# Loading both halves of a weight tile in one 1 MB transfer, with the raw weight buffers joined into three pairs

## The chip, the cores and the metric

The kernel runs on one core of one Trainium2 chip. Its time is that of the slowest (here the only) core in device microseconds, from one launch with all inputs in HBM to all outputs in HBM. Three runs of the kernel before gave 1528.47, 1528.53 and 1528.87 us; the median is 1528.53 us.

## The reference

Two decoder layers are applied to 288 token rows: 256 new rows of a prompt and 8 x 4 rows of running sequences, with the same weights. Everything is float32.

```python
def layer(x, l, ...):
    x = x + 0.5 * swiglu(rms_norm(x, ffn1_norm[l]), ffn1_w1[l], ffn1_w3[l], ffn1_w2[l])   # 1024 -> 2816 -> 1024
    h = rms_norm(x, mix_norm[l]) @ w_in[l]                     # 1024 -> 6144 columns, read by all three branches
    a_u, a_v, b_q, b_k, b_v, c_q, gates = jnp.split(h, IN_SPLITS, axis=-1)
    y_a = gelu(a_u) * chunk_spatial_gate(layer_norm(gelu(a_v)))
    y_b = moba_attention(rope(b_q), rope(b_k), b_v, paged cache)
    y_c = cross_attention(c_q, mem_k, mem_v)
    x = x + (g_a * (y_a @ w_a) + g_b * (y_b @ w_b) + g_c * (y_c @ w_c)) @ w_o
    x = x + 0.5 * swiglu(rms_norm(x, ffn2_norm[l]), ffn2_w1[l], ffn2_w3[l], ffn2_w2[l])
```

The outputs are the final norm of x and the new keys, values, memory keys and values and gate rows of both layers.

## The kernel before

**Units.** Every weight matrix is cut into tiles of up to 1024 rows by 256 columns, and each tile into two halves, the units. A unit is 128 partitions by 4 row blocks by 256 columns (512 KB); where a tile has 768 or 512 rows, a unit has 3 or 2 row blocks. `layer_units` (its list is `UNITS`) writes the order of a layer's 224 units: 68 of the first FFN, 8 of the memory projection, 24 of `w_in` for queries, keys, values and the gated branch, 40 of gates and branch outputs, 8 of `w_b_out`, 8 of `w_o`, 68 of the second FFN. Units are numbered from 0 to 447 over both layers.

**The way of a unit.** SyncE (SP) loads unit n into raw buffer n % 6 (`load`). ScalarE (ACT) copies it, rounded, into one of four high buffers (`hi`, L831). VectorE (DVE) writes the rest, raw minus high, over the raw data (`lo`, L1158; `wlo` is the same memory as `wraw`). TensorE (PE) multiplies high x high, high x low and low x high: 24 matmuls for a unit of four row blocks (`half`, L476). After its last matmul it raises `w_used`. Four things wait for that count: SP loads unit n when unit n - 6 has been used, ACT rounds unit n when unit n - 4 has been used, and both evacuations of a finished tile start there.

**What sets the order.** Each engine has one program order written out by hand. On ACT the rounding of a later unit stands at a fixed place among the other work; when its data isn't there, everything behind it on ACT waits too. Three places matter below. In the branch part, `slot(i)` is `hi` of the layer's unit 88 + i, so `slot(10)` rounds unit 98 and `slot(14)` unit 102:

```python
            slot(10)
            act.wait_ge(xc_ready, L + 1)
            act.activation(lnsq[:], gv[:], ACT.Square, scale=SGU ** -0.5).then_inc(lnsq_ready, 1)
            ...
            deviation(f"ln2.{L}")
...
            slot(14)
            rows_out("vn", rows_a, 2)
```

`deviation` takes the root that the normalisation of `gv_T` on DVE needs (L1426, L1428), whose rows PE then transposes (L537) and ACT copies back (`rows_out`, L973). In the gate part, step n's sigmoid of unit u stands behind `hi(u + 3)`; the third place is the sigmoid of the layer's unit 123 (branch C, tile 2) behind `hi` of unit 126. The next gate tile uses the same PSUM bank, so PE cannot start unit 126 before that sigmoid is done.

**Pages.** Caches come in as quads of four 256 KB pages. 24 quads of a layer are issued by SP between two weight loads (`quads_after`, at `load_after(q)`), 16 by GpSimd (POOL) on its own queue. Rows of a weight unit are 4 KB per partition, rows of a page are 2 KB.

Of the kernel before, what the change touches and what calls it, by code (L numbers as in the profile page):

```python
# [6 lines left out]
F32 = mybir.dt.float32  # L7
F32R = mybir.dt.float32r
# [5 lines left out]
P = 128  # L14
# [8 lines left out]
W = 256  # L23
# [57 lines left out]
LAYER_UNITS = 224  # L81
# [21 lines left out]
def step_unit(n):  # L103

    return U_GA + sum(1 if k in "ABC" else 2 for k, _, _ in STEPS[:n])


def layer_units():

    def tile(name, t, k0=0, nk=KD):  # L110
        return [(name, t, k0 + h * nk // 2, nk // 2) for h in range(2)]

    def ffn(f):
        u = []
        for i in range(UP):
            u += tile(f"ffn{f}_w1", i) + tile(f"ffn{f}_w3", i)
        for t in range(12):
            u += tile(f"ffn{f}_w2", t // 3, 8 * (t % 3), DOWN_NK[t % 3])
        return u

    def gate(kind, g):
        return tile("w_in", g + (GATE0 + "ABC".index(kind) * D) // W)

    u = ffn(1)
    assert len(u) == U_MEM
    for t in range(4):
        u += tile("w_mem_kv", t)
    for t in [4, 5, 6, 7] + SLOT_TILES:
        u += tile("w_in", t)
    assert len(u) == U_GA  # L130
    for kind, g, h in STEPS:
        u += gate(kind, g)[h:h + 1] if kind in "ABC" else tile(f"w_{kind}_out", g, 0, 4)
    assert len(u) == U_BRB
    for g in range(4):
        u += tile("w_b_out", g, 0, 4)
    for t, h in WO_ORDER:
        u += tile("w_o", t)[h:h + 1]
    assert len(u) == U_FFN2
    u += ffn(2)
    assert len(u) == LAYER_UNITS  # L140
    return u


UNITS = layer_units()
N_UNITS = DEPTH * LAYER_UNITS
NR, NH = 6, 4


def kh_of(n):
    return UNITS[n % LAYER_UNITS][3]  # L150

RES = 48
RES_FFN, RES_MEM, RES_Q, RES_K, RES_TILES, RES_GATE = 13, 2, 1, 1, 4, 4
# [22 lines left out]
def load_after(q):  # L178

    if q in FIRST_LOAD:  # L180
        return FIRST_LOAD[q]
    prev = max(p for p in range(q) if HOMES[p] == HOMES[q])
    free = quad_unit(prev)
    if q == Q_V + 3:
        free = step_unit(13) - 1
    if q == Q_V + 4:
        free = step_unit(14) - 1
    return free + NR


def by_pool(q):
    return 8 <= q < Q_MK or q >= Q_V + 8
# [8 lines left out]
def user_before(L, q):  # L201

    prev = [p for p in range(q) if HOMES[p] == HOMES[q]]
    if prev:
        return QUADS * L + prev[-1] + 1
    return (QUADS * (L - 1) + max(p for p in range(QUADS) if HOMES[p] == HOMES[q]) + 1) if L else 0
# [53 lines left out]
def build(nc, A):  # L260
# [3 lines left out]
    def at(name, shape, dt, offset):  # L264
        return nc.alloc_sbuf_tensor_at(name, shape, dt, offset=offset)

    def room(nbytes):
        o = base[0]
        base[0] += (nbytes + 31) // 32 * 32
        assert base[0] <= 229344, base[0]  # L270
        return o

    def sb(name, shape, dt=F32):
        return at(name, shape, dt, room(int(np.prod(shape[1:])) * 4))

    def sem(name):
        return st.enter_context(nc.semaphore(name))


    wraw, wlo = [], []  # L280
    for u in range(NR):
        o = room(4 * W * 4)
        wraw.append(at(f"wraw{u}", [P, 4, W], F32, o))
        wlo.append(at(f"wlo{u}", [P, 4, W], F32R, o))
    whi = [sb(f"whi{u}", [P, 4, W], F32R) for u in range(NH)]
    x = sb("x_T", [P, KD, T])
    work_at = base[0]
# [80 lines left out]
    raw_loaded = [sem(f"raw_loaded{u}") for u in range(NR)]  # L368
    first_hi, first_lo = sem("first_unit_hi"), sem("first_unit_lo")
    hi_done, lo_done, w_used = sem("hi_done"), sem("lo_done"), sem("w_used")  # L370
# [62 lines left out]
    wt = {n: A[n] for n in TILED}  # L433
# [376 lines left out]
    def _(act):  # L810
# [8 lines left out]
        def hi(n):  # L819

            if n >= N_UNITS:
                return
            kh = kh_of(n)
            act.wait_ge(raw_loaded[n % NR], 16 * (n // NR + 1))
            if n >= NH:
                act.wait_ge(w_used, n - NH + 1)
            if n == 0:
                act.activation(whi[0][:, 0:2, :], wraw[0][:, 0:2, :], ACT.Copy).then_inc(first_hi, 1)
                act.activation(whi[0][:, 2:4, :], wraw[0][:, 2:4, :], ACT.Copy).then_inc(hi_done, 1)
                return  # L830
            act.activation(whi[n % NH][:, 0:kh, :], wraw[n % NR][:, 0:kh, :], ACT.Copy).then_inc(hi_done, 1)  # L831
# [805 lines left out]
    @block.sync  # L1637
    def _(sp):
        nc.disable_value_cache = True

        def load(n):

            name, t, k0, kh = UNITS[n % LAYER_UNITS]
            if n >= NR:
                sp.wait_ge(w_used, n - NR + 1)
            sp.dma_start(wraw[n % NR][:, 0:kh, :], wt[name][n // LAYER_UNITS, t][:, k0:k0 + kh, :])\
                .then_inc(raw_loaded[n % NR], 16)

        def ids_of(i, n):

            G, j = i // 8, i % 8
            _, ids = nc.values_load_multi_w_load_instructions(
                ptab[0:1, :].rearrange("o (b j) -> o b j", j=8)[:, 4 * G:4 * G + 4, j:j + n],
                engines=(mybir.EngineType.SP,), min_val=0, max_val=A["cache_k"].shape[1] - 1)
            return [[ids[e * n + k] for e in range(4)] for k in range(n)]

        held = []

        def quad(L, q):

            b = HOMES[q]
            if user_before(L, q):
                sp.wait_ge(quad_used, user_before(L, q))
            if Q_MK <= q < Q_V:
                cache, i = (cache_mk, q - Q_MK) if q < Q_MV else (cache_mv, q - Q_MV)
                src = [cache[L, 4 * (i // 2) + e, i % 2] for e in range(4)]
            else:
                cache, i = (cache_k, q - Q_K) if q < Q_MK else (cache_v, q - Q_V)
                ids = held[i]
                src = [cache[L, ids[e]] for e in range(4)]  # L1670
            for e in range(4):
                sp.dma_start(page[b][e][:], src[e]).then_inc(page_loaded[b], 16)

        def quads_after(L, n):
            for q in range(QUADS):
                if not by_pool(q) and load_after(q) == n:
                    quad(L, q)

        for g in range(4):
            sp.dma_start(x[:, 2 * g:2 * g + 2, :], A["x_T"][:, 2 * g:2 * g + 2, :]).then_inc(ld_x[g], 16)  # L1680
            if g == 0:
                sp.dma_start(gains[:], A["gains"]).then_inc(ld_gain, 16)
            if g < 2:
                load(g)
        for n in range(2, NR):
            load(n)
        sp.wait_ge(ld_page, 16)
        for L in range(DEPTH):
            b = LAYER_UNITS * L
            for n in range(b + NR if L == 0 else b + NR, b + U_MEM):  # L1690
                load(n)
                if L == 0 and n == 10:
                    sp.dma_start(memn[:], A["mem_T"]).then_inc(ld_mem, 16)
                if L == 0 and n == 14:
                    sp.dma_start(cst[:], A["const"]).then_inc(ld_const, 16)
                if L == 0 and n in (16, 20, 24, 28):
                    held += ids_of(n // 2 - 8, 2)
                if n == b + 28:
                    sp.dma_start(sgb[:], A["sgu_b"][L].unsqueeze(0).broadcast_to([P, 4, P])).then_inc(ld_sb, 16)
                    sp.dma_start(wmT[:], A["sgu_w"][L]).then_inc(ld_sw, 16)  # L1700
                if L and n == b + load_after(0):
                    sp.wait_ge(out_vn, 16 * L)
                    sp.wait_ge(out_v, 32 * L)
                quads_after(L, n - b)
            for n in range(U_MEM, U_BRB):
                load(b + n)
                if n == load_after(2):
                    sp.wait_ge(w_used, b + U_MEM)
                if n == load_after(Q_V + 3):
                    sp.wait_ge(w_used, b + step_unit(13))  # L1710
                if n == load_after(Q_V + 4):
                    sp.wait_ge(*fill(f"O11.{L}"))
                quads_after(L, n)
            for n in range(b + U_BRB, b + LAYER_UNITS + NR):
                if n < N_UNITS:
                    load(n)
        for g in range(4):
            if g == 2:
                sp.wait_ge(y_pool, 1)
            else:  # L1720
                sp.wait_ge(nf_ready, 4 * DEPTH + min(g, 2) + 1)
            sp.dma_start(A["y"][:, 2 * g:2 * g + 2, :], yout[:, 2 * g:2 * g + 2, :]).then_inc(out_y, 16)
        sp.wait_ge(out_y, 64)
# [136 lines left out]
```

## Time and profile before

| | |
|---|---|
| median of three runs | 1528.53 us |
| the profiled execution, its own time | 1527.0 us |
| its span, first to last instruction | 1525.3 us |
| granted TensorE clock, mean | 0.995 |
| PE busy | 1492.3 us (98%) |
| DVE busy, ACT busy, POOL busy | 897.7, 705.5, 103.9 us |
| moved by DMA | 316.03 MB |

The span is 1.7 us shorter than the profiled execution's time, and that execution is 1.5 us shorter than the median of the runs. Busy time of an engine counts its own instructions, not the time in which it waits for a semaphore. A matmul's end is modelled, so a busy PE isn't shown to run at its peak.

### The profile page before, as it was taken

How to read it: one execution, taken by the hardware profiler on the slowest of the kernel's cores; microseconds unless marked ns; L12 is line 12 of the kernel's file. 1: busy time of each engine (PE TensorE's matmuls, PEld its weight loads, DVE VectorE, ACT ScalarE, POOL GpSimd, SP SyncE). 2: the span in 40 equal slices, each digit the busy share in tenths (PEclk: the TensorE clock that was granted, in tenths of full speed). 3: DMA queues.
4: the chain of work that ended last, by engine and by line, in shares of the span. 5: the costliest groups of instructions: out<-in, count | busy, mean ns of one | idle time of the engine just before them, and what ended most of it. 6: DMA issues, size and time to landing. Idle time of an engine off the chain costs nothing. (4 is left out here: it accounts for less than half of the span.)

```text
span 1525.3 us, 28869 instructions
## 1 busy us (share of the span) xinstructions
PE 1492.3 (98%) x12100; PEld 1440.4 (94%) x12100; DVE 897.7 (59%) x1207; ACT 705.5 (46%) x938; POOL 103.9 (7%) x198
## 2 busy tenths in 40 slices
PE   7999999999999999999999999999999999999996
PEld 7999999998878999999999999999988889999995
DVE  6676446656744775555565654665656537655543
ACT  6544335446643454443444443544565435544342
POOL 0000001140012000000000000023100210000000
PEclk9999999999999999999999999999999999999998
DMA  6555659794698544455555466688856955444551
GB/s 241 183 180 190 190 173 322 259 358 155 215 342 292 168 159 165 163 165 162 170 166 176 166 201 181 222 288 301 314 194 208 357 190 199 159 165 162 159 165 66
DMA packets 107026, 316.03 MB, mean 207 GB/s; under 512 B 13392, under 2 KB 13392, under 8 KB 106768
## 3 DMA queue, kind: packets, MB, share of 16 engines
q1 hardware_dynamic: 94320, 273.67, 54.0%
q0 software_dynamic: 12576, 40.51, 7.3%
q8 instruction: 96, 1.57, 0.4%
q14 instruction: 34, 0.28, 0.1%
HBM read 306.00 MB, written 5.77 MB: 204 GB/s over the span
## 5 line engine op out<-in xcount | busy, mean ns | idle before, releaser
L1158 DVE TENSOR_TENSOR wlo<-wraw,whi 128x1024 fp32r<-128x1024 f32 (+2 forms) x447 | 511.0, 1148 | 516.6 <-ACT whi L831 514.9
L476 PE MATMUL res<-norm_hi,whi 128*128 128x288 f32 x2176 | 652.1, 300 | 13.6 <-DVE wlo L1151 7.9
L476 PE MATMUL res<-norm_lo,whi 128*128 128x288 f32 x2176 | 643.3, 296 | 0.0
L831 ACT ACTIVATE whi<-wraw 128x1024 fp32r<-128x1024 f32 (+2 forms) x447 | 441.3, 993 | 433.5 <-PE res L476 361.6
L476 PE MATMUL res<-norm_hi,wlo 128*128 128x288 f32 x2176 | 641.2, 295 | 0.0
L476 PEld LDWEIGHTS res<-norm_hi,whi 128*128 128x128 f32 x2176 | 409.1, 188 | 25.4 <-issue 8.8
L476 PEld LDWEIGHTS res<-norm_hi,wlo 128*128 128x128 f32 x2176 | 411.0, 189 | 0.0
L476 PEld LDWEIGHTS res<-norm_lo,whi 128*128 128x128 f32 x2176 | 410.0, 188 | 0.5
L476 PE MATMUL res<-h_hi,whi 128*128 128x288 f32 x1024 | 304.3, 297 | 1.3 <-DVE h_lo L1597 0.8
L476 PE MATMUL res<-h_lo,whi 128*128 128x288 f32 x1024 | 302.1, 295 | 0.0
L476 PE MATMUL res<-h_hi,wlo 128*128 128x288 f32 x1024 | 301.3, 294 | 0.0
L476 PEld LDWEIGHTS res<-h_hi,whi 128*128 128x128 f32 x1024 | 191.9, 187 | 4.9 <-DVE h_lo L1597 1.7
L476 PEld LDWEIGHTS res<-h_hi,wlo 128*128 128x128 f32 x1024 | 192.8, 188 | 0.0
L476 PEld LDWEIGHTS res<-h_lo,whi 128*128 128x128 f32 x1024 | 192.2, 188 | 0.0
L909 ACT ACTIVATE h_hi<-hf 128x576 fp32r<-128x576 f32 x44 | 30.2, 687 | 96.5 <-DVE hf L1246 96.5
L894 ACT ACTIVATE sil<-scaled 128x576 f32<-128x576 f32 x44 | 30.1, 685 | 84.6 <-DVE scaled L1220 84.6
L1736 POOL MEMSET q_blockdiag<- 128x512 f32 x8 | 4.0, 529 | 581.5 <-DVE h_lo L1205 580.6
L1072 ACT ACTIVATE probs_T<-gb 128x384 f32<-128x384 f32 (+1 forms) x24 | 12.6, 524 | 53.9 <-PE gb L537 53.9
L1220 DVE TENSOR_TENSOR scaled<-res,rstd 128x576 f32<-128x576 f32 x44 | 33.1, 753 | 0.1
L1242 DVE TENSOR_TENSOR scaled<-sil,rstd 128x576 f32<-128x576 f32 x44 | 33.1, 752 | 0.0
L1205 DVE TENSOR_TENSOR h_lo<-hf,h_hi 128x576 fp32r<-128x576 f32 x44 | 33.1, 752 | 0.0
L1246 DVE TENSOR_TENSOR hf<-scaled,res 128x576 f32<-128x576 f32 x44 | 32.8, 747 | 0.0
(221 smaller groups left out, 1096.7 us busy)
## 6 DMA issues: line engine op xcount, KB each, us to landing
wraw<-in_ffn_w SPq DMA_DIRECT2D x240, 512.0 KB, 3.5
wraw<-in_w_in SPq DMA_DIRECT2D x96, 512.0 KB, 5.6
wraw<-in_ffn_w SPq DMA_DIRECT2D x32, 384.0 KB, 3.3
page_Q<-in_cache_k POOLq DMA_DIRECT2D x48, 256.0 KB, 6.0
page_Q<-in_cache_k SPq DMA_DIRECT2D x40, 256.0 KB, 5.8
page_Q<-in_cache_v SPq DMA_DIRECT2D x40, 256.0 KB, 5.2
wraw<-in_w_mem_kv SPq DMA_DIRECT2D x16, 512.0 KB, 3.4
page_Q<-in_cache_v POOLq DMA_DIRECT2D x32, 256.0 KB, 6.8
```

Of the source, the lines that this page charges most:

```text
L476: mm = pe.matmul(res[:, 2 * s + c, 0:n], w_, m_, start=begin and k == 0 and j == 0, stop=end and k == kh - 1 and j == 2)
L831: act.activation(whi[n % NH][:, 0:kh, :], wraw[n % NR][:, 0:kh, :], ACT.Copy).then_inc(hi_done, 1)
L894: act.activation(sil[:], scaled[:], ACT.Silu).then_inc(sil_ready, 1)
L909: act.activation(hh[:, 2 * i:2 * i + 2, :], hf[:], ACT.Copy).then_inc(hh_ready, 1)
L1072: act.activation(ptp[(n - 1) % 2][:, 0:k, :], bk(nm)[:, 0:k * P].rearrange("p (k m) -> p k m", k=k), ACT.Copy)\
L1158: dve.tensor_tensor(wlo[n % NR][:, 0:kh, :], wraw[n % NR][:, 0:kh, :], whi[n % NH][:, 0:kh, :].bitcast(F32), ALU.subtract).then_inc(lo_don ...
L1205: dve.tensor_tensor(hl[:, 2 * i:2 * i + 2, :], hf[:], hh[:, 2 * i:2 * i + 2, :].bitcast(F32), ALU.subtract)\
L1220: dve.tensor_tensor(scaled[:], rs(0), both(rstd[:]), ALU.mult).then_inc(evac[0], 1)
L1242: step(dve.tensor_tensor(scaled[:], sil[:], both(rstd[:]), ALU.mult))
L1246: dve.tensor_tensor(hf[:], scaled[:], rs(1), ALU.mult).then_inc(evac[1], 1)
L1736: i = pool.memset(qbd[g][:], 0.0)
```

## The change

The six raw buffers become three pairs of adjacent buffers, and where two consecutive units from number 6 on are the two halves of one tile with four row blocks each, the first of them being even, one `dma_start` loads both: 128 partitions by 8 row blocks, 1 MB, with rows of 8 KB. The condition is `in_one`. The joint load waits until both buffers are free, that is for the count at which the second half alone was loaded before (`w_used` at n - 4 instead of n - 5 for the even unit). 173 of the 224 pairs of units are loaded so; the others (units 0 to 5, tiles with 6 or 4 row blocks, tiles whose halves don't stand side by side in the order) keep two loads. The semaphore of the even buffer is raised once for both halves, and a table, `RAW_COUNT`, says which semaphore and count `hi` waits for.

```diff
+def in_one(n):
+    a, b = UNITS[n % LAYER_UNITS], UNITS[(n + 1) % LAYER_UNITS]
+    return n >= NR and n % 2 == 0 and a[:2] == b[:2] and a[3] == 4 and b[3] == 4 and b[2] == a[2] + 4
+
+def raw_count():
+    count, of = [0] * NR, []
+    for n in range(N_UNITS):
+        if n % 2 and in_one(n - 1):
+            of.append(of[-1])
+        else:
+            count[n % NR] += 1
+            of.append((n % NR, count[n % NR]))
+    return of
...
-    for u in range(NR):
-        o = room(4 * W * 4)
-        wraw.append(at(f"wraw{u}", [P, 4, W], F32, o))
-        wlo.append(at(f"wlo{u}", [P, 4, W], F32R, o))
+    for u in range(NR // 2):
+        o = room(8 * W * 4)
+        wraw2.append(at(f"wraw_pair{u}", [P, 8, W], F32, o))
+        lo2 = at(f"wlo_pair{u}", [P, 8, W], F32R, o)
+        for h in range(2):
+            wraw.append(wraw2[u][:, 4 * h:4 * h + 4, :])
+            wlo.append(lo2[:, 4 * h:4 * h + 4, :])
...
-            act.wait_ge(raw_loaded[n % NR], 16 * (n // NR + 1))
+            act.wait_ge(raw_loaded[RAW_COUNT[n][0]], 16 * RAW_COUNT[n][1])
...
+            if n % 2 and in_one(n - 1):
+                return
+            if in_one(n):
+                sp.wait_ge(w_used, n - NR + 2)
+                sp.dma_start(wraw2[n % NR // 2][:], wt[name][n // LAYER_UNITS, t][:, k0:k0 + 8, :]).then_inc(raw_loaded[n % NR], 16)
+                return
             if n >= NR:
                 sp.wait_ge(w_used, n - NR + 1)
```

On SP, in the branch part of a layer, the units 94 to 101 stand between a value of the key cache and the first pages of the memory keys. Before:

```order
L1672 DMA page_Q0_3_113<-in_cache_k 128x512
L1646 DMA wraw4_57<-in_w_in 128x1024 [waits w_used]
L1646 DMA wraw5_59<-in_w_in 128x1024 [waits w_used]
L1646 DMA wraw0_49<-in_w_in 128x1024 [waits w_used]
L1646 DMA wraw1_51<-in_w_in 128x1024 [waits w_used]
L1646 DMA wraw2_53<-in_w_in 128x1024 [waits w_used]
L1646 DMA wraw3_55<-in_w_in 128x1024 [waits w_used]
L1646 DMA wraw4_57<-in_w_in 128x1024 [waits w_used]
L1646 DMA wraw5_59<-in_w_in 128x1024 [waits w_used]
L1672 DMA page_Q3_0_122<-in_cache_mem_k 128x512 [waits quad_used]
```

And with the change (unit 98 is the first half of the third of these loads):

```order
L1703 DMA page_Q0_3_107<-in_cache_k 128x512
L1673 DMA wraw_pair2_53<-in_w_in 128x2048 [waits w_used]
L1673 DMA wraw_pair0_49<-in_w_in 128x2048 [waits w_used]
L1673 DMA wraw_pair1_51<-in_w_in 128x2048 [waits w_used]
L1673 DMA wraw_pair2_53<-in_w_in 128x2048 [waits w_used]
L1703 DMA page_Q3_0_116<-in_cache_mem_k 128x512 [waits quad_used]
```

Eight loads became four, and each takes the wait of the second half; the pages keep their places.

On SP, in the gate part, the units 126 to 131 stand behind the last page quad that SP issues in a layer. Before:

```order
L1672 DMA page_Q1_3_117<-in_cache_v 128x512
L1646 DMA wraw0_49<-in_w_in 128x1024 [waits w_used]
L1646 DMA wraw1_51<-in_w_in 128x1024 [waits w_used]
L1646 DMA wraw2_53<-in_w_c_out 128x512 [waits w_used]
L1646 DMA wraw3_55<-in_w_c_out 128x512 [waits w_used]
L1646 DMA wraw4_57<-in_w_in 128x1024 [waits w_used]
L1646 DMA wraw5_59<-in_w_in 128x1024 [waits w_used]
```

And with the change:

```order
L1703 DMA page_Q1_3_111<-in_cache_v 128x512
L1673 DMA wraw_pair0_49<-in_w_in 128x2048 [waits w_used]
L1677 DMA wraw_pair1_51<-in_w_c_out 128x512 [waits w_used] x2
L1673 DMA wraw_pair2_53<-in_w_in 128x2048 [waits w_used]
L1673 DMA wraw_pair0_49<-in_w_in 128x2048 [waits w_used]
```

The two halves of unit 126's tile are one load; the `w_c_out` halves behind it stay two loads of 256 KB.

## Rows read from the trace of the kernel before

**Rows 1.** The page: busy us, share of the span, instructions.

```profile
PE 1492.3 (98%) x12100; PEld 1440.4 (94%) x12100; DVE 897.7 (59%) x1207; ACT 705.5 (46%) x938; POOL 103.9 (7%) x198
```

**Rows 2.** Waits of PE: total us, times, longest us; the two longest of eight.

```profile
PE res L476 <- DVE wlo L1151: 7.9, 1, 7.9
PE res L476 <- ACT gate_sigmoid L842: 5.1, 2, 2.5
```

**Rows 3.** Waits of all engines: ACT's rounding, for PE and for loads.

```profile
ACT whi L831 <- PE res L476: 361.6, 206, 7.2
ACT whi L831 <- DMA wraw<-in_w_in: 57.8, 25, 6.4
```

**Rows 4.** A window of the second FFN: busy us (count) per engine, PEclk, DMA share, GB/s.

```profile
620.00:690.00 70.00, 70.00 (x527) 70.00 (x526) 41.19 (x45) 29.66 (x33) 0.00 (x0) 1.00 0.51 161
```

**Rows 5.** The page's DMA issues, FFN units: KB each, median us from issue to landing.

```profile
wraw<-in_ffn_w SPq DMA_DIRECT2D x240, 512.0 KB, 3.5
```

**Rows 6.** All DMA issues: the one load of 1 MB with 8 KB rows.

```profile
memn_T<-in_mem_T SPq DMA_DIRECT2D x1, 1024.0 KB, 6.9
```

**Rows 7.** Timeline of ACT in the FFN: start, us, instruction [idle before, releaser].

```profile
653.85 1.04 ACT L831 ACTIVATE whi<-wraw 128x1024 fp32r<-128x1024 f32 x1
656.57 1.06 ACT L831 ACTIVATE whi<-wraw 128x1024 fp32r<-128x1024 f32 x1 [1.68 <-PE res L476]
```

**Rows 8.** Timeline of DVE, the same stretch.

```profile
654.93 1.23 DVE L1158 TENSOR_TENSOR wlo<-wraw,whi 128x1024 fp32r<-128x1024 f32 x1 [1.70 <-ACT whi L831]
```

**Rows 9.** Timeline of ACT, first layer, unit 98 and the root behind it.

```profile
320.56 1.06 ACT L831 ACTIVATE whi<-wraw 128x1024 fp32r<-128x1024 f32 x1 [1.37 <-DMA wraw<-in_w_in]
...
327.54 0.50 ACT L848 ACTIVATE square_sums<-gb,eps 128x288 f32<-128x288 f32 x1
```

**Rows 10.** Timeline of DVE behind that root.

```profile
331.62 1.45 DVE L1428 TENSOR_SCALAR gv_T<-gv_T,gains 128x288 f32<-128x288 f32 x4
```

**Rows 11.** Timeline of PE: the transposes that read gv_T.

```profile
334.17 0.49 PE L537 MATMUL gb<-consts,gv_T 128*128 128x128 f32 x3
```

**Rows 12.** DMA issues in 314.9 to 315.1 us: unit 99.

```profile
wraw<-in_w_in SPq DMA_DIRECT2D x1, 512.0 KB, 8.2
```

**Rows 13.** DMA queues in 322 to 325 us: packets, MB, share (q0 POOL's, q1 SP's).

```profile
q0 software_dynamic: 200, 0.65, 56.4%
q1 hardware_dynamic: 147, 0.54, 46.1%
```

**Rows 14.** Timeline of ACT, second layer, unit 102 of the layer and what follows.

```profile
1091.96 1.06 ACT L831 ACTIVATE whi<-wraw 128x1024 fp32r<-128x1024 f32 x1 [5.80 <-DMA wraw<-in_w_in]
1092.92 0.57 ACT L973 ACTIVATE rows_a<-gb 32x512 f32<-32x512 f32 x1
```

**Rows 15.** DMA issues in 1082.3 to 1082.6 us: unit 103 of that layer.

```profile
wraw<-in_w_in SPq DMA_DIRECT2D x1, 512.0 KB, 10.9
```

**Rows 16.** Timeline of PE: the products that read those rows.

```profile
1093.75 0.35 PE L651 MATMUL gb<-sgu_wT,rows_a 128*128 128x128 f32 x1
```

**Rows 17.** First layer, the same copy on ACT.

```profile
343.43 0.57 ACT L973 ACTIVATE rows_a<-gb 32x512 f32<-32x512 f32 x1
```

**Rows 18.** First layer, the same products on PE.

```profile
345.58 0.38 PE L651 MATMUL gb<-sgu_wT,rows_a 128*128 128x128 f32 x1
```

**Rows 19.** Timeline of ACT, second layer, unit 126 of the layer and the sigmoid.

```profile
1203.77 1.06 ACT L831 ACTIVATE whi<-wraw 128x1024 fp32r<-128x1024 f32 x1 [6.36 <-DMA wraw<-in_w_in]
...
1206.14 0.65 ACT L842 ACTIVATE gate_sigmoid<-res 128x576 f32<-128x576 f32 x1
```

**Rows 20.** DMA issues in 1194.2 to 1194.35 us: unit 127 of that layer.

```profile
wraw<-in_w_in SPq DMA_DIRECT2D x1, 512.0 KB, 12.3
```

**Rows 21.** Timeline of PE: the first matmul of unit 126, second layer.

```profile
1207.29 0.40 PE L476 MATMUL res<-norm_hi,whi 128*128 128x288 f32 x1
```

**Rows 22.** First layer, the same sigmoid on ACT.

```profile
454.57 0.65 ACT L842 ACTIVATE gate_sigmoid<-res 128x576 f32<-128x576 f32 x1
```

**Rows 23.** First layer, the same first matmul on PE.

```profile
457.66 0.40 PE L476 MATMUL res<-norm_hi,whi 128*128 128x288 f32 x1
```

More of the change, by code:

```diff
@@ L150, in kh_of @@
     return UNITS[n % LAYER_UNITS][3]
+def in_one(n):
[10 more added lines that the diff above has]
+    return of
+RAW_COUNT = raw_count()
 RES = 48
@@ L280, in build @@
     wraw, wlo = [], []
-    for u in range(NR):
-        o = room(4 * W * 4)
-        wraw.append(at(f"wraw{u}", [P, 4, W], F32, o))
-        wlo.append(at(f"wlo{u}", [P, 4, W], F32R, o))
+    wraw2 = []
+    for u in range(NR // 2):
[5 more added lines that the diff above has]
+            wlo.append(lo2[:, 4 * h:4 * h + 4, :])
     whi = [sb(f"whi{u}", [P, 4, W], F32R) for u in range(NH)]
```

## The prediction

> **What bounds the kernel now.** I read the page's busy times first. PE is busy for 1492.3 of 1525.3 us [rows 1]; 33.0 us are left. The waits of PE say what they are: 7.9 us before the first matmul, and 5.1 us in two waits for a sigmoid on ACT [rows 2]; no wait of PE names a load. A load shows up one engine earlier: ACT waits for `w_in` units before rounding them, 25 times, 57.8 us in all, and it waits 361.6 us for PE at the same line [rows 3]. So ACT runs ahead of PE, and a late load costs ACT's lead, not PE's time, as long as the lead lasts. A window of pure FFN shows PE busy all the time at full clock with DMA engines at 0.51 [rows 4]: faster loads give nothing there. I therefore look for places where a load that arrives later eats the whole lead.
>
> **What goes.** 173 load instructions leave SP, which is not on PE's path. Startup (units 0 to 5) is untouched. Nothing that PE, ACT or DVE executes changes, so their busy time stays. I count no gain.
>
> **What the joint wait costs in the FFNs.** In the window, 527 matmuls took 70.00 us, 0.133 us each, so a unit of 24 takes 3.19 us [rows 4]. An even unit n was rounded at 653.85 and unit n + 1 at 656.57, when PE released it, that is at the end of unit n - 3 [rows 7]. PE therefore starts unit n two units later, near 662.9. The joint load is issued at the end of unit n - 5, two units before 656.55, at 650.2. How long 1 MB takes in an FFN the trace does not show often. It cannot land before 512 KB did, 3.5 us [rows 5]; the one load of 1 MB with 8 KB rows took 6.9 us, with other loads beside it [rows 6]. So the pair lands between 653.7 and 657.1. Rounding takes 1.04 to 1.06 us and the low part 1.23 us [rows 7, 8]: unit n is ready by 659.4 at the latest, 3.5 us before PE wants it, and unit n + 1 a rounding later with 3.2 us more. All FFN units: 0 us, covered by PE's own work on the four units ahead. The cover is gone when 1 MB takes more than 6.9 + 3.5 = 10.4 us.
>
> **What it costs in the mixing part.** There the DMA engines are full. In such a stretch both halves were queued already, and the pair's data can't be complete before the second half's were, unless the weights' queue gets a larger share. So ACT's rounding of the even half moves from the landing of the first half to about that of the second. What stands behind that rounding on ACT moves with it. Three places have little room.
>
> *Place A, unit 98.* First layer: ACT rounded it at 320.56, as soon as it landed, and the root for the gate norm came at 327.54, with ACT busy in between [rows 9]. DVE's scaling behind that root ended at 331.62 + 1.45 = 333.07 [rows 10], and PE's transposes of the result began at 334.17 [rows 11]: 1.1 us of room. Unit 99, issued at 315.0, took 8.2 us [rows 12], so it landed at 323.2. Landing of the pair: at best 320.6, at worst 323.2. In this stretch POOL's queue moved 0.65 MB and SP's 0.54 MB, in near equal packets [rows 13], as if rows of the two queues took turns. An 8 KB row in such turns would give the weights two thirds instead of one half: 0.5 MB at 0.40 MB/us, which is (0.65 + 0.54) / 3, takes 2.0 instead of 2.65 us. Over one and a half halves in competition that is 1.0 us. I take 322.2, nearer to the upper end: 1.6 us late, less 1.1 of room, 0.5 us for PE; ends 0 and 1.5. The Trainium skill (DMA: Bandwidth & Descriptors, "Queues, rings and completion order") says that each DMA engine goes round the queue rows that have work, a packet at a time; the trace's near equal shares agree. By it the joint load gains on the pages as taken here; if a packet held a fixed number of bytes, place A would cost its upper end. In the second layer I take the same 0.5 us, but place B follows in the same stretch and PE then arrives there later by as much, so only the larger of the two counts.
>
> *Place B, unit 102, second layer.* ACT rounded it at 1091.96 on landing, and the copy of the last gate rows behind it ended at 1092.92 + 0.57 = 1093.49 [rows 14]. PE's products with these rows began at 1093.75 [rows 16], 0.26 us later. Unit 103, issued at 1082.3, took 10.9 us [rows 15]: 1093.2. The pair delays the copy by 1.24 us, PE by 1.0 us; ends 0 and 1.5 (place A's upper end, if that is larger). I take 1.0, since little stood behind the pair in the queue for it to overtake. In the first layer the copy ended at 343.43 + 0.57 = 344.00 [rows 17] and PE began at 345.58 [rows 18]; 1.58 us of room against some 1.2 us: nothing.
>
> *Place C, unit 126, second layer.* ACT rounded it at 1203.77 on landing after 6.36 us of idling, then ran the sigmoid that frees the bank, which ended at 1206.14 + 0.65 = 1206.79 [rows 19]; PE began the unit at 1207.29 [rows 21], 0.5 us of room. Unit 127, issued at 1193.9, took 12.3 us [rows 20]: 1206.2. If the pair lands then, the sigmoid is 2.4 us late and PE loses 1.9; with the better share over the second half alone (0.65 us), 1.3 us. I take 1.3; ends 0 and 1.9. In the first layer the sigmoid ended at 455.22 [rows 22] and PE began at 457.66 [rows 23]: 2.4 us of room, as much as the largest delay of place C, so 0.
>
> **Sum.** 0.5 (A, first layer) + 1.0 (B) + 1.3 (C) = 2.8 us; ends 0 and 1.5 + 1.5 + 1.9 = 4.9. The profiled execution took 1527.0 us (span 1525.3 and 1.7 around it), so its successor would take 1529.8; it lay 1.5 us under the median of the runs, so against the median I add the 2.8 to 1528.5: 1531.3. Some of these delays may be met by PE's own later arrival, since a stall at one place gives room at the next; I round down to 1531.0.
>
> Within 0.2% of 1528.53, which is 3.06 us, a measurement of this kernel cannot tell a change, so 1531.0 counts as no change, and the boundary to slower, 1531.6, lies close above it.
>
> **Rivals.** *Slower, by the pages' competition.* If a longer row gives no larger share, each place costs its upper end, 4.9 us: 1533.4. One more place of this kind, with an ACT instruction behind a rounding and little room on PE, would add 1 to 2 us. For it: ACT's 25 waits for `w_in` [rows 3], each of them a rounding that now waits for two halves. Against it: the near equal turns of rows 13. It decides from 1.6 us of extra stall over the sum's first 1.5.
>
> *Slower, by lost depth in the FFNs.* A 1 MB load that took 11.4 us there would cost 1 us at each joint pair, more than 100 us in all. Against it: 6.9 us [rows 6] with DMA engines half idle [rows 4]. I give it 0.02.
>
> *No stall at all.* The pairs land when the first half used to, or ACT's other work is moved without PE noticing: 1528.5. For it: PE has no wait that names a load. Against it: the three margins of 0.26, 0.5 and 1.1 us are smaller than the distance between the halves' landings.
>
> *Faster.* Full-size transfers move more per us where the DMA engines are full, loads land sooner, and ACT's waits shrink. PE could gain at most its 5.1 us behind the sigmoids [rows 2], 1523.4, and only if those came from loads. The Trainium skill (the same page, "Rules for kernel authors") recommends 1 MiB and more per transfer for bandwidth; rows 13 move 0.40 MB/us with smaller ones already.
>
> **How the numbers follow.** Small stalls at the three places, 0.5 to 3.0 us: 0.43. No stall: 0.13. Slower by the upper ends or a further place: 0.37. FFN depth: 0.02. Faster: 0.05. No change is thus 0.56, which I put at 0.55 for the boundary's nearness, slower 0.40, faster 0.05. The range runs from no stall, 1528.3, to the upper ends and one further place, 1534.8; what is left out is the FFN case, most of the faster one and a longer tail of stalls.
>
> **What the profile after would show.** FFN windows with PE busy throughout and no new wait of PE for `wlo` L1158: the depth holds. ACT's rounding of unit 98, 102 and 126 near the landings of the second halves, less up to 1 us: the moved landing holds. New idle time of PE before L537 (first layer), L651 and L476 (second layer) of 0.5, 1.0 and 1.3 us: the three terms. I am wrong if PE waits at other places than these, if FFN units wait for loads, or if PE's busy time itself changes.

## The result: 1549.2 us, 1.36% slower

The changed kernel took 1549.2 us (median of four runs, 1547.58 to 1549.84) against 1528.5 us for the kernel before on the same chip: a ratio of 1.0136, 95% interval 1.0123 to 1.0148. That is 20.7 us more, where I had forecast 2.5 us and a range up to 1534.8. The profiled execution (1549.84 us, the longest of the four) has a span of 1548.2 us, 22.9 us over the one before.

The first row of the page after, which answers to [rows 1], gives busy us, share and instructions of each engine:

```profile
PE 1501.6 (97%) x12100; PEld 1448.9 (94%) x12100; DVE 890.9 (58%) x1207; ACT 709.5 (46%) x938; POOL 103.8 (7%) x198
```

PE executes the same 12100 instructions, and its busy time rose by 9.3 us. The rest of the 22.9 us, 13.6 us, is idle time. The waits of PE after (total us, times, longest us), beside [rows 2], say where PE idled:

```profile
PE res L501 <- DVE wlo_pair L1176: 8.4, 1, 8.4
PE gb L535 <- DVE work L1212: 7.0, 3, 2.5
PE res L501 <- ACT gate_sigmoid L867: 6.2, 4, 2.5
PE gb L535 <- DVE ln_square L1447: 2.7, 2, 2.1
PE res L501 <- DVE h_lo L1622: 1.9, 4, 1.3
...
PE res L501 <- DVE x_T L1205: 1.0, 1, 1.0
PE gb L562 <- DVE gv_T L1453: 1.0, 1, 1.0
```

The first row is the start. No other row names a load or the low part of a late unit. The new rows name sums and updates on DVE: `work` is the sum of squares of x ahead of a norm, `ln_square` that of the gated branch. A load stands two engines further back. ACT's waits before a rounding show it, beside [rows 3]:

```profile
ACT whi L856 <- DMA wraw_pair<-in_ffn_w: 155.1, 91, 4.9
ACT whi L856 <- PE res L501: 145.8, 141, 5.7
ACT whi L856 <- DMA wraw_pair<-in_w_in: 104.3, 27, 9.1
```

In the FFNs ACT now waits for loads 91 times; it waited for PE there before. A window of the second FFN, beside [rows 4], shows that PE doesn't mind: 528 matmuls in 70 us against 527.

```profile
620.00:690.00 70.00, 70.00 (x528) 70.00 (x527) 41.20 (x44) 30.71 (x33) 0.00 (x0) 1.00 0.46 163
```

The two kinds of load in the FFNs (count, KB each, median us from issue to landing), beside [rows 5]:

```profile
wraw_pair<-in_ffn_w SPq DMA_DIRECT2D x117, 1024.0 KB, 4.8
wraw_pair<-in_ffn_w SPq DMA_DIRECT2D x32, 384.0 KB, 3.5
```

**Where the 22.9 us lie.** I count each unit from the end of the unit before it to the end of its own last matmul, in both traces. Three units grew most: unit 70 of the first layer (3.72 to 7.62 us), unit 2 of the second (3.81 to 7.51) and unit 70 of the second (3.70 to 7.53), together 11.4 us. Each has a sum of squares of x in front of it. In the mixing part units 96 and 98 of the first layer grew by 0.7 and 1.2, unit 96 of the second by 3.6, unit 126 by 1.0 and 0.3, and unit 150 (first layer) and 152 (second) by 1.1 and 1.0: 8.9 us. That is 20.3 us. Most of the rest is at the first units (1.1 us), ahead of any joint load, and at unit 102 of the first layer (1.5 us), which took 7.0 us in the first and 8.5 in the second layer of the kernel before already.

**One of the three places, read along the chain.** Before, unit 70 of the first layer, on ACT and then DVE (start, us, instruction):

```profile
220.31 1.06 ACT L831 ACTIVATE whi<-wraw 128x1024 fp32r<-128x1024 f32 x1 [1.33 <-PE res L476]
```
```profile
221.41 1.23 DVE L1158 TENSOR_TENSOR wlo<-wraw,whi 128x1024 fp32r<-128x1024 f32 x1 [1.17 <-ACT whi L831]
...
223.34 0.82 DVE L1180 SCALAR_TENSOR_TENSOR x_T<-res,x_T 128x288 f32<-128x288 f32 x2
...
227.84 0.46 DVE L1187 TENSOR_TENSOR work<-work 128x288 f32<-128x288 f32 x1
```
```profile
228.45 0.72 PE L510 MATMUL gb<-work,ones 128*128 128x288 f32 x2
```

After, the same instructions:

```profile
223.85 1.06 ACT L856 ACTIVATE whi<-wraw_pair 128x1024 fp32r<-128x1024 f32 x1 [3.73 <-DMA wraw_pair<-in_w_mem_kv]
227.79 0.69 ACT L876 ACTIVATE work<-x_T 128x576 f32<-128x576 f32 x1 [2.88 <-DVE x_T L1205]
```
```profile
224.95 1.22 DVE L1183 TENSOR_TENSOR wlo_pair<-wraw_pair,whi 128x1024 fp32r<-128x1024 f32 x1 [3.57 <-ACT whi L856]
...
226.87 0.82 DVE L1205 SCALAR_TENSOR_TENSOR x_T<-res,x_T 128x288 f32<-128x288 f32 x2
229.46 1.22 DVE L1183 TENSOR_TENSOR wlo_pair<-wraw_pair,whi 128x1024 fp32r<-128x1024 f32 x1 [1.76 <-ACT whi L856]
...
231.38 0.46 DVE L1212 TENSOR_TENSOR work<-work 128x288 f32<-128x288 f32 x1
```
```profile
231.99 0.72 PE L535 MATMUL gb<-work,ones 128*128 128x288 f32 x2 [2.54 <-DVE work L1212]
...
232.79 0.41 PE L501 MATMUL res<-mem_hi,wlo_pair 128*128 128x256 f32 x1
...
236.20 0.28 PE L501 MATMUL res<-mem_hi,whi 128*128 128x256 f32 x1
```

The rounding moves from 220.31 to 223.85 because the pair lands then. DVE's program has the low part of unit 70 ahead of the last update of x, so x moves from 223.34 to 226.87, its squares on ACT follow, and behind them the low part of unit 71 (229.46) and the final addition, which moves from 227.84 to 231.38. Each step is 3.5 us late. PE reached this sum at 228.3 before and went on without a stop. Now it reaches it 1.1 us later (the first units' difference) and idles 2.54 us. Then its matmuls take 0.41 us for 3.4 us, and 0.28 again from 236.2. The windows say why (us, busy of PE, PEld, DVE, ACT, POOL, then granted clock, DMA share, GB/s):

```profile
229.00:232.00 3.00, 0.46 (x5) 0.28 (x4) 2.51 (x4) 2.94 (x5) 0.00 (x0) 1.00 0.56 134
232.00:235.00 3.00, 3.00 (x15) 2.90 (x16) 3.00 (x3) 1.76 (x2) 0.00 (x0) 0.63 0.98 388
235.00:238.00 3.00, 3.00 (x23) 3.00 (x23) 2.78 (x5) 0.84 (x1) 0.00 (x0) 0.80 0.48 180
```

After the idle stretch the clock was at its lower level, 1.2 GHz, for 3.4 us: a stall of 2.54 us cost 3.9. The trace after has five such stretches that the trace before has not: at the three sums, at `ln_square` of the second layer and at unit 102 of the first. At some 1.5 us each they are most of the 9.3 us of risen busy time; the first units have 1.1 us of it.

### The profile page after: what moved, and what is told of

Read it like the earlier page. It is cut to its first block, busy times and chain, and to the rows that moved or that the text cites. A ratio compares the mean times of both kernels' runs of the same rounds, so it can differ in the third digit from the quotient of the medians.

```text
span 1548.2 us, 28696 instructions
## 1 busy us (share of the span) xinstructions
PE 1501.6 (97%) x12100; PEld 1448.9 (94%) x12100; DVE 890.9 (58%) x1207; ACT 709.5 (46%) x938; POOL 103.8 (7%) x198
## 4 chain that ended last, share of the span: by engine, by line
PE 89%; DMA 4%; DVE 3%; ACT 2%; issue 1%; DVEq 0%; SPq 0%; ACTq 0%
PE res L501 79%; PE gb L589 2%; DMA wraw_pair<-in_w_in 2%; PE gb L580 2%; PE res L523 1%; PE gb L562 1%; ACT whi L856 1%; DVE wlo_pair L1183 1%; DMA wraw_pair<-in_w_o 1%; DMA wraw_pair<-in_ffn_w 1%; DMA wraw_pair<-in_w_mem_kv 1%; PE gb L743 0%; PE gb L714 0%; PE gb L735 0%; PE gb L711 0%
## 5 line engine op out<-in xcount | busy, mean ns | idle before, releaser
L1183 DVE TENSOR_TENSOR wlo_pair<-wraw_pair,whi 128x1024 fp32r<-128x1024 f32 (+2 forms) x447 | 507.9, 1147 | 548.4 <-ACT whi L856 545.1
L501 PE MATMUL res<-norm_hi,wlo_pair 128*128 128x288 f32 x2176 | 643.7, 296 | 0.0
L856 ACT ACTIVATE whi<-wraw_pair 128x1024 fp32r<-128x1024 f32 (+2 forms) x447 | 438.5, 995 | 431.4 <-DMA wraw_pair<-in_ffn_w 155.1
L501 PEld LDWEIGHTS res<-norm_hi,wlo_pair 128*128 128x128 f32 x2176 | 413.3, 190 | 0.0
L501 PE MATMUL res<-h_hi,wlo_pair 128*128 128x288 f32 x1024 | 301.2, 294 | 0.0
L501 PEld LDWEIGHTS res<-h_hi,wlo_pair 128*128 128x128 f32 x1024 | 192.8, 188 | 0.0
```

The source lines that it names most:

```text
L501: mm = pe.matmul(res[:, 2 * s + c, 0:n], w_, m_, start=begin and k == 0 and j == 0, stop=end and k == kh - 1 and j == 2)
L1183: dve.tensor_tensor(wlo[n % NR][:, 0:kh, :], wraw[n % NR][:, 0:kh, :], whi[n % NH][:, 0:kh, :].bitcast(F32), ALU.subtract).then_inc(lo_don ...
```

## Experiments

Theory: a joint load brings the even half to ACT later. That costs PE nothing through the unit itself, and costs time where other work that PE wants soon stands behind that rounding on ACT, or behind its low part on DVE. Rivals: the size of the transfer or its rows, a small cost per joint load, contention with the pages.

**Three joint loads only.** `in_one` for units 70 and (second layer) 2:

```diff
-    return n >= NR and n % 2 == 0 and a[:2] == b[:2] and a[3] == 4 and b[3] == 4 and b[2] == a[2] + 4
+    return n >= NR and n % LAYER_UNITS in (2, 70) and a[:2] == b[:2] and a[3] == 4 and b[3] == 4 and b[2] == a[2] + 4
```

> Three joint loads only: units 70 and 71 of both layers and units 2 and 3 of the second layer; the other 170 pairs are two loads again. Theory (what stands behind the late rounding): in the trace of the changed kernel PE idles 2.1 to 2.5 us before the sum of squares at these three places and then runs some 4 us at the lower clock; the units there take 3.9, 3.7 and 3.8 us longer than before. If that is one mechanism of its own, three pairs of 173 cost 11.4 us: 1538 to 1542 us. Rival (every joint pair costs a little, by its transfer): 3 / 173 of the 20.7 us, 0.4 us: 1529 us.

Measured: 1537.29 us against 1526.73 us for the kernel before beside it, ratio 1.0065 (1.0048 to 1.0081): 10.6 us by the medians, 9.9 by the ratio, a little under what I expected. Three loads of 173 carry half of the loss.

```profile
PE gb L535 <- DVE work L1212: 6.9, 3, 2.4
```

**The update of x first.** On ACT and DVE, for the last tile of an FFN:

```diff
+                if t == 11 and 2 * L + f < 2 * DEPTH:
+                    new_x(t // 3, (t // 3) % 2, 3 * L + (1 if f == 1 else 3), gain)
                 hi(u + 4)
...
-                lo(u + 4)
+                x_first = t == 11 and 2 * L + f < 2 * DEPTH
+                if not x_first:
+                    lo(u + 4)
...
+                if x_first:
+                    lo(u + 4)
                 lo(u + 5)
```

> All 173 joint loads stay. Only at the last tile of an FFN (not the last FFN) ACT and DVE do the update of x and its squares ahead of the rounding and the low part of the next even unit, not behind them. Theory (what stands behind the late rounding): DVE can update x when PE has finished the tile, 2.3 us earlier than in the changed kernel, so PE's wait for the sum of squares falls from 2.1 to 2.5 us to under 0.5 us and the lower clock behind it goes: 9 to 11.4 us less than 1549.2, so 1538 to 1540 us. Rival (PE waits because the weights themselves land late, or page loads do): the units are as late as before, 1547 to 1551 us.

Measured: 1539.11 us, ratio 1.0087 (1.0066 to 1.0109). With all 173 joint loads in place, an order of instructions gives back 10.1 us against the changed kernel's own runs, which were made at another time; measured from the kernel before beside each, 12.4 us of loss are left of 20.7, so 8.3 us come back, a little less than I expected. The weights land as late as before (ACT waits 93 times for loads of the FFNs, 155.3 us); the three sums wait 1.7 us together, 0.7 at most:

```profile
PE gb L535 <- DVE work L1216: 1.7, 3, 0.7
...
PE gb L535 <- DVE ln_square L1455: 2.2, 2, 1.1
PE res L501 <- DVE x_T L1209: 2.1, 2, 1.1
PE gb L562 <- DVE gv_T L1461: 1.9, 2, 1.0
```

What is left stands mostly in the mixing part, at the same places in both layers, but for unit 126 in the first alone (1.4 us).

**Two loads, issued as late as the joint one.** The kernel before with `in_one` added to it, and one number changed:

```diff
-                sp.wait_ge(w_used, n - NR + 1)
+                sp.wait_ge(w_used, n - NR + (2 if in_one(n) else 1))
```

> The kernel before, with two loads of 512 KB for every pair, but the even half waits for the count of the odd one (one unit later), as the joint load does. It separates the later issue from the larger transfer. Theory: in the FFN the joint load lands 4.8 us after its issue and a load of 512 KB 3.5 us after; so here the rounding of unit 70 is 1.0 us later than before where the joint load makes it 3.5 us later. PE's wait at the three sums is then about 1 us each, too short to bring the clock down, and the mixing part gives 1 to 3 us: 1531 to 1536 us. If the later issue alone is to blame: 1546 to 1551 us. If only the size is: 1528 to 1529.5 us.

Measured: 1535.94 us, ratio 1.0061 (1.0044 to 1.0078): 9.2 us, a little more than I expected against the run beside it (up to 7.5 us over 1528.5). The stalls are where the theory has them, but nearer to 1.5 us than to 1:

```profile
PE gb L516 <- DVE work L1193: 4.4, 3, 1.5
...
PE gb L543 <- DVE gv_T L1434: 1.9, 2, 1.0
```

At unit 70 the rounding started 2.67 us after ACT fell idle, against 1.33 before and 3.73 with the joint load. So the later issue makes somewhat under half of the loss, and waiting for all of the megabyte the rest. Of PE's added idle time it makes about half (6.7 of 13.6 us); the clock stayed at 1.00 after these shorter stalls, so the second part costs more than its share.

**Rows of 4 KB.** One transfer of 1 MB into two buffers that lie apart:

```diff
+    raw_all = at("wraw_all", [P, 2, NR // 2, 4, W], F32, o)
...
+                sp.dma_start(raw_all[:, :, n % NR // 2].rearrange("p h k w -> p h (k w)"),
+                             wt[name][n // LAYER_UNITS, t][:, k0:k0 + 8, :].rearrange("p (h k) w -> p h (k w)", h=2))
```

> The changed kernel, but a pair's two buffers lie apart (three buffers between), so the one transfer of 1 MB has rows of 4 KB instead of 8 KB. Waits, counts and orders are the same. Theory (landing of both halves together): nothing changes at the three sums, 1546 to 1551 us. Rival (long rows hold up the pages and the other queue, or the larger row changes the share of the two queues): the mixing part gets its time back, 5 us or more less, 1540 to 1545 us; in the other direction, if 8 KB rows helped the weights there, up to 3 us more than 1549.2.

Measured: 1550.52 us, ratio 1.0159 (1.0142 to 1.0176), an interval that overlaps that of the changed kernel (1.0123 to 1.0148). The row length isn't the cause. In the FFNs rows of 4 KB landed later, not earlier (beside 4.8 us with 8 KB):

```profile
wraw_all<-in_ffn_w SPq DMA_DIRECT2D x117, 1024.0 KB, 5.2
```

At place A of the prediction the longer row helped in the first layer: unit 98's pair landed 8.7 us after its issue with rows of 8 KB and 10.3 us with 4 KB, and PE waited 0.6 and 2.1 us at `ln_square`. In the second layer both took 10.2 us.

**The rest of the loss.** The x-first kernel, with two loads again where the mixing part has work behind the rounding:

```diff
-    return n >= NR and n % 2 == 0 and a[:2] == b[:2] and a[3] == 4 and b[3] == 4 and b[2] == a[2] + 4
+    return n >= NR and n % 2 == 0 and n % LAYER_UNITS not in (94, 96, 98, 100, 102, 126, 152, 154) and a[:2] == b[:2] and a[3] == 4 and b[3] == 4 and b[2] == a[2] + 4
```

> The update of x ahead of the late rounding, as in the run with x first, and beside it two loads again for the eight pairs per layer whose rounding has other work behind it in the mixing part (units 94 to 103, 126 and 127, 152 to 155); the other 157 joint loads stay. Theory (what stands behind a late rounding): the mixing part's stalls of the run with x first (1.2 + 1.2 + 1.5 + 1.1 in the first layer, 1.1 + 1.2 + 1.0 in the second) go, the three sums keep 0.5 us each: 1.6 us above the kernel before. Rival (a joint load costs something at each of the 157 places, or the clock lost its steadiness): 3 us or more above it.

Measured: 1528.64 us against 1528.3, ratio 1.0008 (0.9999 to 1.0017). The interval ends at 2.6 us, under the rival's 3. And orders untouched, with 2 and 70 in that list too:

> Orders untouched; two loads again for units 2 and 3, 70 and 71 and those eight pairs of each layer. 154 joint loads stay, all with nothing urgent behind their rounding. Theory: no stall is left, within 1 us of the kernel before in either direction. Rival (a cost per joint load): 154 / 173 of what the three sums and the named places don't explain, 3 us or more above it.

Measured: 1527.63 us, ratio 0.9995 (0.9986 to 1.0004). Its 154 joint loads are as late as ever on ACT, and cost nothing:

```profile
ACT whi L856 <- DMA wraw_pair<-in_ffn_w: 154.1, 91, 5.0
ACT whi L856 <- PE res L501: 147.8, 140, 6.9
```

**Eight raw buffers.** With joint loads, and with single ones as the control:

```diff
-NR, NH = 6, 4
+NR, NH = 8, 4
...
-    memn = sb("memn_T", [P, KD, MEM])
+    memn = at("memn_T", [P, KD, MEM], F32, memn_at)
```

> The changed kernel with eight raw buffers (four pairs), so a joint load waits for unit n - 7 instead of n - 5: 6.4 us earlier in an FFN. To make room the memory rows share the memory of its keys and values and are loaded a second time for layer 1 (1 MB more), where their normalisation is left out. Theory (lateness of the even half): it lands 4.8 us after issue, two units earlier than now and so 1.9 us earlier than the first of two loads did; ACT waits for PE again and not for loads in the FFNs, and PE's stalls are gone: within 1.5 us of the kernel before. Rival (size of the transfer, packets, contention): the depth changes nothing about these, and the time stays 8 us or more above it.

> The kernel before with eight raw buffers and the same second load of the memory rows (layer 1 without their normalisation): the control for the run with eight buffers and joint loads. Theory: no wait of PE in the kernel before hung on a load, so within 1 us of it, and the joint loads with eight buffers are no faster than this. Rival (loads did hold up the mixing part before): 2 us or more faster than the kernel before.

Measured: 1526.91 us with joint loads and 1527.33 us with single ones, against 1528.3; ratios 0.9993 (0.9983 to 1.0002) and 0.9997 (0.9988 to 1.0006). Both leave out the normalisation of the memory rows in layer 1, so they measure loads and are no versions to use. The same joint transfers (172 now, as units 6 and 7 belong to the start), issued two units earlier, cost nothing in any place. ACT waits for PE again, with joint loads:

```profile
ACT whi L857 <- PE res L502: 399.5, 228, 7.2
...
ACT whi L857 <- DMA wraw_pair<-in_w_in: 6.1, 2, 3.0
```

**A version faster than both.** The price of a stall with its clock pointed at the two waits of 2.54 us that the kernel before already had [rows 2]. On ACT, the sigmoid of unit 101 stood behind a copy that waits for PE:

```diff
-                            take(u, 0, gsil[k % 2][:], ACT.Sigmoid)
+                            if n != 2:
+                                take(u, 0, gsil[k % 2][:], ACT.Sigmoid)
...
+                    if n == 1:
+                        take(LAYER_UNITS * L + step_unit(1), 0, gsil[0][:], ACT.Sigmoid)
                     wait(fill(nm))
```

> The kernel before, loads untouched; only the sigmoid of unit 101 (gates of branch A, tile 0) moves on ACT ahead of the copy of the first transposed probabilities, which waits for PE. The earlier runs showed that 2.5 us of idle PE at a sum cost 3.8 us, since PE then runs at its lower clock for some us. The two waits of 2.54 us for this sigmoid should have the same price. Theory (an instruction behind another wait on ACT, then the clock): ACT could change its table and take the sigmoid when PE has finished unit 101; PE's wait falls from 2.54 to under 1 us in both layers, and unit 102 of a layer, 7.0 to 8.5 us long, to some 5: 4 to 7 us less than the kernel before. Rival (the change of table starts only once the tile is done, and the copy that now comes later holds PE instead): at most 2 us less.

> The same move of the sigmoid in the kernel with 154 joint loads (two loads where other work stands behind the rounding). Theory: joint loads without lateness cost nothing, so the same 4 to 7 us less than the kernel before, within 1 us of the run without joint loads. Rival (their lateness shows as soon as PE has less idle time to hide it): 2 us or more slower than that run.

Measured: 1520.65 us with the loads of before, 1520.96 us with 154 joint loads, against 1527.6; ratios 0.9955 (0.9941 to 0.9969) and 0.9956 (0.9943 to 0.9970). The row of the sigmoid is gone from PE's waits, and unit 102 takes 4.56 us in both layers. On ACT the table is loaded as soon as the exponential is done, while PE still works on unit 101, whose last matmul starts at 357.14:

```profile
356.54 1.28 ACT L842 ACT_TABLE_LOAD   x1
357.83 0.65 ACT L842 ACTIVATE gate_sigmoid<-res 128x576 f32<-128x576 f32 x1
358.45 0.49 ACT L1075 ACTIVATE probs_T<-gb 128x384 f32<-128x384 f32 x1
```

Joint loads bring nothing in any of these kernels: the gain is the order's.

## Why the prediction was wrong

**The FFN term failed.** I costed all FFN units, and with them those of the memory projection, at 0 us, "covered by PE's own work on the four units ahead". The arrival was right: I had the pair land 3.5 to 6.9 us after its issue, and it took 4.8. The cover was right for the units too: in the FFNs their low parts still ended 1.5 us or more before PE wanted them, and FFN windows are full. But I compared the late rounding with one consumer, PE's use of that unit. I asked what stands behind a rounding only in the mixing part. At the end of an FFN the update of x and its squares stand there, and PE took the resulting sum with no room at all in the kernel before (DVE's addition ended at 228.30, PE began at 228.45). These three places made 11.4 us of some 20. The runs with three joint loads and with x first show it from both sides.

The Trainium skill (SBUF — State Buffer, "The DMA setup-cost knee") gives a transfer a fixed part and one by its bytes, so that a larger transfer moves more per us. The traces agree, with 512 KB in 3.5 us [rows 5] and 1 MB in 4.8: more per us, and each half later. ACT had use only for the second of these two facts.

**A stall's price was left out.** I priced stalls as idle time and wrote that PE's busy time stays; it rose by 9.3 us. After 2.06 to 2.54 us of idling at four sums PE ran at its lower clock for 3.4 us, which added 1.4 to 1.6 us each time. The price isn't fixed: the last section has stalls of that length without it. The profile before could have told me: of its two waits for a sigmoid [rows 2], both about 2.54 us, one was followed by a unit 102 of 7.0 us and the other by one of 8.5; without the wait this unit takes 4.56.

**The mixing part: the mechanism held, the places and sizes didn't.** The sum of three places was 2.8 us, ends 0 and 4.9; the mixing part measured 8.9 us. Of that 1.1 us at unit 150 (first layer) and 1.0 at unit 152 (second) were not on the list: there `h_lo` and an update of x stand behind a low part on DVE, and with two loads at those pairs again the new waits are gone but for 0.2 us.

*Place A.* I forecast 0.5 us before the transposes of `gv_T`. There were 0.97 us in the first layer, and 0.60 us one step earlier, at `ln_square`, whose square on ACT stands directly behind the rounding of unit 98 and which I had passed over. In the second layer that nearer consumer took all of it. After, on ACT, DVE and PE:

```profile
1091.55 1.06 ACT L856 ACTIVATE whi<-wraw_pair 128x1024 fp32r<-128x1024 f32 x1 [5.97 <-DMA wraw_pair<-in_w_in]
1092.52 1.15 ACT L1023 ACTIVATE ln_square<-gv_T 128x1152 f32<-128x1152 f32 x1
```
```profile
1094.57 0.46 DVE L1447 TENSOR_TENSOR ln_square<-ln_square 128x288 f32<-128x288 f32 x1
```
```profile
1095.18 0.72 PE L535 MATMUL gb<-ln_square,ones 128*128 128x288 f32 x2 [2.06 <-DVE ln_square L1447]
```

The upper bound failed here as well. I let the pair land no later than the second half did before. Before, that rounding was at 1068.29; it came 23.26 us later, while PE was 18.44 us later at this point. That is 4.8 us, where the second half's landing (1071.38) allowed 3.1. The two halves of before are issued 3.2 us apart, and the first had been moving meanwhile; the joint load starts with all of it still to move. The run with two late loads, whose halves also start together, bears this out: there the second half landed 10.2 and 10.6 us after its issue in the two layers, against 8.2 and 8.5 before.

*Place B* showed nothing in its layer. The stall at `ln_square` made PE 3.6 us later there, as the prediction had reckoned for a smaller stall. The load is issued later with PE, so that alone gives no room; but the pair landed 6.3 us after its issue, where the second half had taken 10.9 before, and while it was under way POOL's queue moved 0.02 MB, against 0.60 MB beside the second half before. That the queue had emptied during the stall is my reading, not shown. *Place C* was forecast at 1.3 us in the second layer and 0 in the first. It cost 0.27 and 1.0: in the first layer ACT waited 9.07 us for that pair, longer than any wait I had in the trace before.

**The rivals.** "Slower, by the pages' competition" had the right sign and a chance of 0.37, with at most 1534.8. That was luck as to the cause: about half of the loss lies at the three sums at the ends of FFNs, which the rival doesn't have, and the runs with two late loads and with 4 KB rows put that loss on the later issue and on the wait for the whole megabyte. What the pages' competition adds in the mixing part is not separated. "Lost depth in the FFNs" was the right word with the wrong victim: no pair stalled PE for its weights.

## What to carry over

When a load, a copy or any early step on an in-order engine becomes later, list everything queued behind it on that engine, and behind its successor on the next, and compare each with the time at which the bound engine wants it; the consumer of the late data itself may be the one with most room. Merging two transfers saved nothing here, where neither issue nor bandwidth was on PE's path, and it makes the first half wait for the last byte and for the last free buffer: keep it for loads with nothing urgent behind them, or pay with one more pair of buffers. Price a stall of TensorE by the matmuls after it as well, as a price that may or may not fall due.

## What the runs showed of the hardware

Idle time of PE alone did not settle its clock. After 2.07 us of idling in the changed kernel the granted clock was 0.65 in the next 3 us; after 2.06 us at the same sum in the run with three joint loads it stayed at 1.00, and so it did after 2.85 us at the sum of unit 70 (first layer) in the run with rows of 4 KB:

```profile
778.00:781.00 3.00, 2.97 (x14) 2.90 (x15) 3.00 (x3) 2.44 (x3) 0.00 (x0) 0.65 0.69 289
```
```profile
775.00:778.00 3.00, 3.00 (x25) 3.00 (x24) 2.97 (x3) 1.31 (x2) 0.00 (x0) 1.00 0.00 0
```
```profile
231.00:234.00 3.00, 3.00 (x24) 2.90 (x25) 3.00 (x3) 1.55 (x2) 0.00 (x0) 1.00 1.03 405
```

The twelve profiles of this case hold 32 waits of PE of 2.0 to 2.9 us behind the start: the sums that a late load held up and, in ten of them, the two for the sigmoid of unit 101. Of these 32, 20 have a stretch at the lower clock at their end or within 2 us behind it, 12 have none; the wait of 2.54 us for the sigmoid alone has it 11 times out of 20. Of 21 waits of 0.9 to 1.7 us one has it. So one profile of a kernel does not give the price of a stall, and part of the difference between two runs of one kernel can be this; what decides is not shown.

In the run with two late loads PE idled 1.48 us at the sum of unit 70, between full units of 24 matmuls, and the clock stayed at 1.00. The one shorter wait with the lower clock is in the run with the sigmoid first and 154 joint loads: PE idled 1.02 us until 1092.70, after two stretches of narrow products with page quads (128 x 32), and from 1094 on the granted clock was 0.69 and 0.64:

```profile
1094.00:1096.00 2.00, 2.00 (x11) 1.66 (x10) 1.94 (x3) 1.23 (x1) 0.25 (x1) 0.69 0.90 317
1096.00:1099.00 3.00, 3.00 (x17) 3.00 (x16) 2.92 (x15) 1.11 (x5) 0.00 (x0) 0.64 0.77 281
```

It may be that the work before a wait counts as well; one case doesn't show it, and the two waits of 2.06 and 2.07 us above came after the same work.

Left open: in the run with the sigmoid first and 154 joint loads, that wait of 1.02 us was for `rows_a` in the second layer, place B of the prediction, though unit 102 had its two loads there (the first took 13.8 us). One profile doesn't tell a cost of the joint loads around it from chance, and the times of the two kernels agree.
